# Last classic part of the down projection with tokens on the output partitions, the residual transposed between its products, and each token tile stored by itself

## The chip, the cores and the metric

The kernel runs on one core of one Trainium2 chip. The metric is the device time of one execution in microseconds (us), as the median of several runs. The kernel before took 2611.05 us (three runs: 2614.22, 2610.66, 2611.05).

## The reference, cut to what matters

One decoder layer for 512 tokens of width 2048, all in float32: an input projection, windowed attention and a gated short convolution, their merge, a cross-attention into 256 memory tokens, a SwiGLU mixer, and a last RMS norm. The lines that the change touches:

```python
h = h + memory_cross_attention(rms_norm(h, g_xattn[l]), mem_n, w_xq[l], w_xkv[l], w_xo[l])
# inside it: s = einsum('bshd,bmhd->bhsm', q, k) * X_HEAD_DIM ** -0.5
h = h + swiglu(rms_norm(h, g_ffn[l]), w_gate_up[l], w_down[l])   # (silu(g) * u) @ w_down, D_FF = 5632
return rms_norm(h, g_final)    # h * rsqrt(mean(h*h) + 1e-6) * g_final
```

## The kernel before, in words

**Arithmetic.** Almost every product is done in three fp32r matmuls: each operand is split into a high part (a copy that ScalarE, ACT, writes as fp32r) and a low part (the rest, which VectorE, DVE, subtracts), and hi·hi + hi·lo + lo·hi are added up in PSUM. `hi()` and `lo()` do this for weights in four slots of 128x512 (`w_hi`, `w_lo`, `SPL = 4`). The raw weights come in loads of 512 KB into four buffers (`raw`); a load waits until the low parts of the load four before it are done (`s_lo`). ACT and DVE each work through one list in order, so an instruction that waits holds everything behind it. SyncE (SP) issues the loads, also in order; GpSimd (POOL) issues spills and the accumulating stores of the residual. The large projections use a Strassen-like scheme of seven products on halves (`products`, `cycle_products`, L1025 and L1036), the rest the classic form (`columns`, L785 to L787; `rows`, L800 to L802).

**Start.** The tokens are transposed by TensorE (PE), tile by tile: call m of `x_in` (L839) transposes four 128x128 blocks into a bank; ACT copies it (`x_hi`, L1235), DVE subtracts (`x_lo`, L1853). Eight of these stand before the first product; ACT and DVE do six of them, then the first weight, then two more. The first product waits for all eight (`s_xlo`).

**Cross-attention.** The queries `xq_t` and keys `kx` are held in plain f32. Sixteen scores of 128x256 (`x_scores`, L1112) are each one f32 matmul, which the trace shows as two records. They stand between the products of the value projection.

**Down projection.** The 44 tiles of the hidden dimension are taken as 4 + 16 + 4 + 16 + 4. The parts of 4 are classic (`classic_part`), the parts of 16 go through the seven products (`down[0]`, `down[1]`). For the latter SP loads blocks of weights into `braw` (two buffers; the first lies over `raw`). Results of all parts but the last are added to `acc_dram` by accumulating stores that POOL issues. The last classic part has its features on the output partitions, 16 tiles of 128 features x 512 tokens, in four groups (`G_LAST` to `G_LAST + 3`) of four banks.

**End.** SP reloads the summed residual (`acc_end`, four loads of 1 MB) and POOL loads the final gain (`gfin`, 1 MB). DVE adds each finished bank to its tile (`last_sum`, L2664), ACT squares it, DVE adds the squares (L2318); four small matmuls sum them over the partitions (L816), ACT and DVE form the reciprocal root (L1812 to L1818, L1248), then 64 transposes on PE (L1200) turn the sum to tokens on partitions, DVE multiplies by root and gain from PSUM (L2695, 16 times) and SP stores eight pieces of 512 KB (L685).

Of the kernel before, what the change touches and what calls it, by code (L numbers as in the profile page):

```python
# [176 lines left out]
def build(nc, x, mem, g_mix, w_in, conv_w, sinks, w_attn_o, w_conv_o, w_out, g_xattn, g_mem,  # L177
          w_xq, w_xkv, w_xo, g_ffn, w_gate_up, w_down, g_final, rope, out):
    with ExitStack() as ctx:
# [45 lines left out]
        kx = at("kx", 168 * KB, [P, XH, NMEM])  # L225
# [16 lines left out]
        y_out = at("y_out", 0, [P, TT, D])  # L242
# [71 lines left out]

        def evicted(n, j):

            return (gate_t, up_t)[j // 2][:, n % 2, j % 2, :]
# [17 lines left out]
        X_STEPS = {-3: (6, 7), 7: (8, 9), 8: (10, 11), 11: (12, 13), 12: (14, 15)}  # L335
# [18 lines left out]
        s_mem = sem("mem_loaded")  # L354
        s_gfin = sem("gfinal_loaded")
# [48 lines left out]
        s_mtlo = sem("mem_lo_ready")  # L404
        s_xs = sem("xscores_done")
# [10 lines left out]
        s_shi = sem("combination_hi_ready")  # L416
# [5 lines left out]
        s_gn = sem("gate_scaled")  # L422
        s_un = sem("up_scaled")
# [39 lines left out]
        s_mshi = sem("mixer_combination_hi_ready")  # L463
# [12 lines left out]
        s_fT = sem("final_transposed")  # L476
        s_y = sem("y_ready")
        s_out = sem("out_stored")
# [8 lines left out]
        def _(sp):  # L487
# [162 lines left out]

            for i in range(3):
# [4 lines left out]
                if i == 2:  # L656
                    for c in range(2):
                        for p in range(2):
                            sp.wait_ge(s_add[p], 32 * (9 + c))
                        sp.wait_ge(ffn.used, down[1].number("P6", DB - 1) + 2)  # L660
                        sp.dma_start(acc_end[:, 4 * c:4 * c + 4, :], acc_dram[c]).then_inc(s_ald[c], 16)
                    for p in range(RAW, 8):
                        down_load(i, p)
                    for c in range(2, 4):
                        for p in range(2):
                            sp.wait_ge(s_add[p], 32 * (9 + c))
                        sp.wait_ge(ffn.used, down[1].number("P7", DB - 1) + 2)
                        sp.dma_start(acc_end[:, 4 * c:4 * c + 4, :], acc_dram[c]).then_inc(s_ald[c], 16)
                    continue
                for n in (0, 2, 1, 3):  # L670
                    quad_load(i, n)
                for p in range(RAW, 8):
                    down_load(i, p)
                    if p == 5:
                        for q in (1, 0, 2, 3):
                            down_block_load(i, 1, q)
                for q in range(4):
                    down_block_load(i, 0, q)
                for b in range(2, DB):
                    for q in (1, 0, 2, 3):  # L680
                        down_block_load(i, b, q)
            for m in range(2 * TT):
                t, f = m // 2, slice((m % 2) * (D // 2), (m % 2 + 1) * (D // 2))
                sp.wait_ge(s_y, 2 * (m + 1))
                sp.dma_start(out[0, t * P:(t + 1) * P, f], y_out[:, t, f]).then_inc(s_out, 16)  # L685
            sp.wait_ge(s_out, 16 * 2 * TT)
# [3 lines left out]
        def _(pool):  # L690
# [77 lines left out]
            pool.dma_start(gfin[:, :], g_final.partition_broadcast(P)).then_inc(s_gfin, 16)  # L768
# [3 lines left out]
        def _(pe):  # L772
# [69 lines left out]
            for m in range(8):  # L842
                x_in(m)
                if m == 3:
# [13 lines left out]
            for g in range(2):  # L858
                for k in range(KT):
                    wait_block(B_QKV + KT * g, 0, None, k)  # L860
                    if k == 0:
                        pe.wait_ge(s_xlo, 8 * g + 8)
# [243 lines left out]
            def x_scores(u):  # L1106
                h, t = divmod(u, TT)
                if u == 0:
                    pe.wait_ge(s_freed, 4 * G_XK + 4)
# [64 lines left out]
            for i in range(3):  # L1174
                for c in range(4):
                    g = G_DOWN + 4 * i + c
                    free = blocks_freed((ffn, *down)[i], c) if c < 2 else freed(g)
                    for k in range(CK):
# [4 lines left out]
                        columns(banks(g), k, CK, act[:, 0, :], act[:, 1, :], wait_bank=free)  # L1183
                if i < 2:
                    products(down[i])


            FB = banks(G_LAST)
            square_sums(FB[0], 3 * KT)
            for m in range(TT * 4):  # L1190
                t, kg = divmod(m, 4)
                bk = bank[(m + 1) % 8] if FB is A else bank[(m + 5) % 8]
                if m >= 7:
                    pe.wait_ge(s_y, m - 7 if m > 7 else 1)
# [1525 lines left out]
```

## Time and profile before

| | |
|---|---|
| runs of the kernel | 2614.22, 2610.66, 2611.05 us |
| the profiled execution's own time | 2611.81 us |
| its span, first to last instruction | 2610.0 us |
| mean granted TensorE clock | 0.999 |
| PE busy | 2589.1 us (99%) |
| DVE, ACT, POOL busy | 2039.8 (78%), 1326.6 (51%), 96.8 us (4%) |
| DMA | 360.02 MB, mean 138 GB/s |

A start time in a row below counts from the start of the span. The duration of a matmul is its latency; two that follow each other overlap, so the pace is read from the distance of their starts. A bracket at the end of a timeline row gives the idle time of the engine before it and what ended it. The profiled execution took 1.8 us more than its span and lies 0.76 us above the median.

### The profile page before, as it was taken

How to read it: one execution, taken by the hardware profiler on the slowest of the kernel's cores; microseconds unless marked ns; L12 is line 12 of the kernel's file. 1: busy time of each engine (PE TensorE's matmuls, PEld its weight loads, DVE VectorE, ACT ScalarE, POOL GpSimd, SP SyncE). 2: the span in 40 equal slices, each digit the busy share in tenths (PEclk: the TensorE clock that was granted, in tenths of full speed). 3: DMA queues.
4: the chain of work that ended last, by engine and by line, in shares of the span. 5: the costliest groups of instructions: out<-in, count | busy, mean ns of one | idle time of the engine just before them, and what ended most of it. 6: DMA issues, size and time to landing. Idle time of an engine off the chain costs nothing.

```text
span 2610.0 us, 36693 instructions
## 1 busy us (share of the span) xinstructions
PE 2589.1 (99%) x13649; PEld 2229.1 (85%) x13649; DVE 2039.8 (78%) x3362; ACT 1326.6 (51%) x2457; POOL 96.8 (4%) x154
## 2 busy tenths in 40 slices
PE   8999999999999999999999999999999999999998
PEld 7888888888888888888888888888888888888887
DVE  5556876654999974456879999999999998888886
ACT  6334554444555553435565555555555556456453
POOL 0000000000000000000000000000000001011100
PEclk9999999999999999999999999999999999999999
DMA  7332222545544573234434343343443467678664
GB/s 230 102 89 81 81 76 87 188 144 167 149 144 142 165 250 130 90 95 131 162 113 122 117 137 110 118 137 109 121 134 110 124 204 174 135 193 198 132 176 151
DMA packets 391715, 360.02 MB, mean 138 GB/s; under 512 B 11804, under 2 KB 314996, under 8 KB 388980
## 3 DMA queue, kind: packets, MB, share of 16 engines
q1 hardware_dynamic: 373620, 292.67, 37.9%
q0 software_dynamic: 17920, 65.02, 9.0%
q8 instruction: 109, 1.79, 0.3%
q14 instruction: 66, 0.54, 0.1%
HBM read 304.17 MB, written 53.48 MB: 137 GB/s over the span
## 4 chain that ended last, share of the span: by engine, by line
PE 96%; DVE 2%; DMA 1%; ACT 0%; issue 0%; DVEq 0%; ACTq 0%
PE bank L1025 35%; PE bank L1036 18%; PE bank L785 11%; PE bank L786 11%; PE bank L787 11%; PE bank L800 2%; PE bank L802 2%; PE bank L801 2%; PE bank L906 0%; DMA braw<-in_w_down_dram 0%; DMA h_both<-hidden_spilled 0%; DVE y_out L2695 0%; DVE s_both L2584 0%; PE bank L839 0%; PE bank L894 0%; PE bank L1140 0%
## 5 line engine op out<-in xcount | busy, mean ns | idle before, releaser
L2100 DVE TENSOR_TENSOR w_lo<-braw,w_hi 128x512 fp32r<-128x512 f32 x504 | 322.9, 683 | 21.6 <-ACT w_hi L1404 21.6
L1404 ACT ACTIVATE w_hi<-braw 128x512 fp32r<-128x512 f32 x504 | 285.5, 625 | 52.5 <-PE bank L1036 19.6
L1827 DVE TENSOR_TENSOR w_lo<-raw,w_hi 128x512 fp32r<-128x512 f32 x224 | 154.2, 690 | 201.8 <-ACT w_hi L1219 201.1
L1219 ACT ACTIVATE w_hi<-raw 128x512 fp32r<-128x512 f32 x224 | 141.5, 632 | 287.5 <-PE bank L787 282.6
L1829 DVE SCALAR_TENSOR_TENSOR w_lo<-raw,par,w_hi 128x512 fp32r<-128x512 f32 x208 | 155.1, 750 | 149.1 <-ACT w_hi L1219 148.0
L2100 DVE TENSOR_TENSOR h_both<-braw,h_both 128x512 fp32r<-128x512 f32 x392 | 250.9, 683 | 2.7 <-ACT h_both L1404 2.5
L1219 ACT ACTIVATE w_hi<-raw,par 128x512 fp32r<-128x512 f32 x208 | 149.3, 721 | 193.5 <-PE bank L787 122.4
L1404 ACT ACTIVATE h_both<-braw 128x512 fp32r<-128x512 f32 x392 | 221.9, 625 | 23.6 <-PE bank L1036 17.6
L785 PE MATMUL bank<-h_both,w_hi 128*128 128x512 f32 x576 | 228.9, 397 | 0.3 <-DVE v_c L1986 0.3
L786 PE MATMUL bank<-h_both,w_hi 128*128 128x512 f32 x576 | 224.8, 390 | 0.0
L787 PE MATMUL bank<-h_both,w_lo 128*128 128x512 f32 x576 | 224.6, 390 | 0.0
L1025 PE MATMUL bank<-s_both,w_hi 128*128 128x512 f32 x896 | 220.6, 391 | 0.0
L1025 PE MATMUL bank<-s_both,h_both 128*128 128x512 f32 x896 | 220.5, 391 | 0.0
L1427 ACT ACTIVATE snap_b<-bank 128x512 f32<-128x512 f32 x68 | 40.7, 599 | 323.7 <-PE bank L1025 321.7
L1025 PEld LDWEIGHTS bank<-s_both,h_both 128*128 128x128 f32 x896 | 164.7, 188 | 31.8
L1025 PEld LDWEIGHTS bank<-s_both,w_hi 128*128 128x128 f32 x896 | 164.5, 188 | 31.7
L1025 PE MATMUL bank<-h_both 128*128 128x512 f32 x672 | 167.5, 391 | 0.0
L1025 PE MATMUL bank<-h_both,w_hi 128*128 128x512 f32 x672 | 167.4, 391 | 0.0
L1025 PEld LDWEIGHTS bank<-h_both,w_hi 128*128 128x128 f32 x672 | 122.8, 188 | 23.3
L1025 PEld LDWEIGHTS bank<-h_both 128*128 128x128 f32 x672 | 122.6, 188 | 23.1
L787 PEld LDWEIGHTS bank<-h_both,w_lo 128*128 128x128 f32 x576 | 108.1, 188 | 23.7
L1036 PE MATMUL bank<-s_both,w_lo 128*128 128x256 f32 x896 | 125.5, 283 | 1.3 <-DVE w_lo L2100 1.3
(303 smaller groups left out, 5605.1 us busy)
## 6 DMA issues: line engine op xcount, KB each, us to landing
braw<-in_w_gate_up_dram SPq DMA_DIRECT2D x160, 512.0 KB, 5.2
raw<-in_w_in_dram SPq DMA_DIRECT2D x80, 512.0 KB, 3.7
braw<-in_w_in_dram SPq DMA_DIRECT2D x64, 512.0 KB, 5.0
braw<-in_w_down_dram SPq DMA_DIRECT2D x64, 512.0 KB, 6.0
raw<-in_w_out_dram SPq DMA_DIRECT2D x32, 512.0 KB, 3.8
raw<-in_w_down_dram SPq DMA_DIRECT2D x24, 512.0 KB, 5.6
hidden_spilled<-up_t POOLq DMA_DIRECT2D x44, 256.0 KB, 5.6
raw<-in_w_attn_o_dram SPq DMA_DIRECT2D x16, 512.0 KB, 3.8
```

Of the source, the lines that this page charges most:

```text
L785: pe.matmul(o_, w_hi[:, s, c], hi, start=(k == 0), stop=False)
L786: pe.matmul(o_, w_hi[:, s, c], lo, start=False, stop=False)
L787: mm = pe.matmul(o_, w_lo[:, s, c], hi, start=False, stop=(k == n - 1))
L800: pe.matmul(bk[j][:, :], hi[:, c], w_hi[:, s, :], start=(k == 0), stop=False)
L801: pe.matmul(bk[j][:, :], hi[:, c], w_lo[:, s, :], start=False, stop=False)
L1025: mm = pe.matmul(r, st.slot_hi[st.slot(n + half)][:, q, :], both, start=(not on and half == 0 and q == 0), stop=(on_last == "wide" and hal ...
L1036: mm = pe.matmul(r[:, 1, :], st.slot_lo[st.slot(n + half)][:, q, :], u_h, start=False, stop=(on_last == "narrow" and half == 1 and q == 3) ...
L1219: nc.scalar.activation(w_hi[:, s, :], raw[:, n % RAW, (b0 + k) % 2, :], ACT.Copy, scale=sc).then_inc(s_hi, 1)
L1404: nc.scalar.activation(st.slot_hi[s], weights(name, b)[:, 4 * half:4 * half + 4, :], ACT.Copy).then_inc(st.hi, 1)
L1827: nc.vector.tensor_tensor(w_lo[:, s, :], src, w_hi[:, s, :], ALU.subtract).then_inc(s_lo, 1)
L1829: nc.vector.scalar_tensor_tensor(w_lo[:, s, :], src, g[:, k:k + 1], w_hi[:, s, :], ALU.mult, ALU.subtract).then_inc(s_lo, 1)
L2100: nc.vector.tensor_tensor(st.slot_lo[s], weights(name, b)[:, 4 * half:4 * half + 4, :], st.slot_hi[s], ALU.subtract).then_inc(st.lo, 1)
```

## The change

The core of it, the end of the kernel:

```diff
-        y_out = at("y_out", 0, [P, TT, D])
+        y_out = at("y_out", 96 * KB, [P, TT, D])
+        end_hi = at("end_hi", 0, [P, 3 * CK, 512], F32R)
+        end_lo = at("end_lo", 24 * KB, [P, 3 * CK, 512], F32R)
+        END = [(t, c) for c in range(4) for t in range(2)] + [(t, c) for t in (2, 3) for c in range(4)]
+        END_LAST = {6: 0, 7: 1, 11: 2}
+        END_ROWS = {4: (0,), 5: (1,), 6: (2,), 7: (3,), 8: (4,), 9: (5,), 10: (6, 7), 11: (8, 9), 12: (10, 11, 12), 13: (13, 14), 14: (15,)}
...
+            def end_products(i):          # PE
+                t, c = END[i]
+                if i < 6:
+                    ((first, 0), (first, 1), (first, 2), (second, 2), (first, 3), (second, 0))[i][0]((0, 1, 2, 2, 3, 0)[i])
+                else:
+                    pe.wait_ge(s_freed, 4 * G_LAST + i - 5)
+                ts = slice(t * P, (t + 1) * P)
+                for k in range(CK):
+                    wait_block(B_DOWN + CK * (8 + c), 0, None, k)
...
+                    pe.matmul(sums[i % 6][:, :], act[:, 0, ts], hi, start=(k == 0), stop=False)
+                    pe.matmul(sums[i % 6][:, :], act[:, 0, ts], lo, start=False, stop=False)
+                    mm = pe.matmul(sums[i % 6][:, :], act[:, 1, ts], hi, start=False, stop=(k == CK - 1))
+                mm.then_inc(s_done, 1)
+            def end_rows(i):              # PE
+                t, c = END[i]
+                pe.wait_ge(s_ald[c], 16)
+                if i < 2:
+                    second(3 if i == 0 else 1)
+                else:
+                    pe.wait_ge(s_rows, i - 1)
+                for q in range(4):
+                    mm = pe.transpose(rows_[i % 2][:, q * P:(q + 1) * P], acc_end[:, 4 * c + q, t * P:(t + 1) * P], ident[:, :])
+                mm.then_inc(s_fT, 1)
+            for i in range(16):
+                end_products(i)
+                for r in END_ROWS.get(i, ()):
+                    end_rows(r)
...
+            for i in range(16):           # ACT; before it: 12 copies into end_hi and the root's table
+                rows_copy(i)
+                if i:
+                    rows_square(i - 1)
+                if i - 1 in END_LAST:
+                    root(5 + END_LAST[i - 1], ...)
+                if i - 2 in END_LAST:
+                    for c in range(4):
+                        rows_scale(END_LAST[i - 2], c)
+            rows_square(15)
+            root(8, rcol[:, 3:4], rtm[:, 3:4])
+            for c in range(2):
+                rows_scale(3, c)
...
+            for i in range(16):           # DVE; before it: 12 subtractions into end_lo, wait for gfin
+                rows_sum(i)
+                if i:
+                    dve.wait_ge(s_sqr, 2 * KT + i)
+                    link(rows_gain(i - 1, y_part(i - 1)))
+                if i - 1 in END_LAST:
+                    rows_rstd(END_LAST[i - 1])
+            rows_gain(15, tile4[:, 3, :])
+            dve.wait_ge(s_sqr, 2 * KT + 16)
+            rows_rstd(3)
+            dve.wait_ge(s_rcol, 7)
+            nc.vector.tensor_scalar(y_part(14), y_part(14), rcol[:, 3:4], None, ALU.mult).then_inc(s_y3, 1)
+            nc.vector.tensor_scalar(y_part(15), tile4[:, 3, :], rcol[:, 3:4], None, ALU.mult).then_inc(s_y3, 1)
...
+            for t in range(TT - 1):       # SP
+                sp.wait_ge(s_y, 4 * t + 4)
+                sp.dma_start(out[0, t * P:(t + 1) * P, :], y_out[:, t, :]).then_inc(s_out, 16)
+            for c in (2, 0, 3, 1):        # four stores of 256 KB for the last tile
```

`rows_copy(i)` copies the transposed residual of piece i (128 tokens x 512 features) from PSUM to `y_out`, `rows_sum(i)` adds the finished bank, `rows_square(i)` squares it with a row sum, `rows_gain(i)` multiplies it by `gfin`, `rows_rstd(t)` forms the reciprocal root of one token tile, `rows_scale(t, c)` multiplies a piece by it. A transposed piece goes into one of two banks, and `end_rows(i)` waits until `rows_copy(i - 2)` is done. A product from the seventh on waits for `rows_sum(i - 6)`.

The other edits: SP issues the residual's reloads behind the weight loads of the last part (weight load 4; 5, residual 0; 6, residual 1; 7, residual 2; residual 3), where before residual 0 and 1 stood ahead of weight loads 4 to 7. In the two earlier classic parts, the loads of block 1 of the following stage, which stood between weight loads 5 and 6, now stand behind those of block 0. At the start four of the eight `x_hi`, `x_lo` stand before the first weight and the other four behind one weight each (`X_FIRST`); the first product waits for five, and each fourth k for one more; the gains' transpose stands behind the second `x_in` in place of the fourth. In the cross-attention ACT and DVE split the queries and the keys into high and low parts (`xq_hi`, `xq_lo`, `kx_hi`, `kx_lo`; four 128x512 and four 128x256 on each engine) and a score is three fp32r matmuls:

```diff
-                pe.matmul(B[u % 4][:, 0:NMEM], xq_t[:, h, t * P:(t + 1) * P], kx[:, h, :],
-                          start=True, stop=True).then_inc(s_xs, 1)
+                pe.matmul(o_, xq_hi[:, h, q], kx_hi[:, h, :], start=True, stop=False)
+                pe.matmul(o_, xq_hi[:, h, q], kx_lo[:, h, :], start=False, stop=False)
+                pe.matmul(o_, xq_lo[:, h, q], kx_hi[:, h, :], start=False, stop=True).then_inc(s_xs, 1)
```

ACT's four `kx_hi` stand behind its second weight of the value projection, DVE's four `kx_lo` where the four copies `kx` stood, behind its third weight. Four semaphores are folded into others with their counts shifted.

## Rows read from the trace of the kernel before

**Rows 1.** Page, part 1: busy time and share of the span.
```profile
PE 2589.1 (99%) x13649; PEld 2229.1 (85%) x13649; DVE 2039.8 (78%) x3362; ACT 1326.6 (51%) x2457; POOL 96.8 (4%) x154
```
**Rows 2.** Waits of PE after 20 us (us in total, times, longest), the two longest.
```profile
PE bank L816 <- DVE ssq L2318: 3.5, 1, 3.5
PE bank L1036 <- DVE w_lo L2100: 1.3, 1, 1.3
```
**Rows 3.** Timeline (start, duration, engine), PE: first and last product of the part.
```profile
2545.73 0.40 PE L785 MATMUL bank<-s_res,w_hi 128*128 128x512 f32 x1
...
2589.65 0.39 PE L787 MATMUL bank<-s_res,w_lo 128*128 128x512 f32 x1
...
2594.72 8.57 PE L1200 MATMUL bank<-ident,acc_end 128*128 128x128 f32 x64
```
**Rows 4.** Timeline, the end: DVE; then SP's stores (first and last start).
```profile
2594.89 0.16 DVE L1812 TENSOR_SCALAR rtm<-bank 128x4 f32<-128x4 f32 x1 [1.41 <-PE bank L816]
...
2596.33 10.63 DVE L2695 SCALAR_TENSOR_TENSOR y_out<-bank,rcol,gfin 128x512 f32<-128x512 f32 x16
...
L685 SPq DMA_DIRECT2D out_dram<-y_out x8: 332/332/338, 2597.8 to 2607.0; - x8
```
**Rows 5.** Timeline, PE: eight transposes between two products at the start.
```profile
25.45 0.39 PE L802 MATMUL bank<-w_hi,h_both 128*128 128x512 f32 x1
...
25.68 1.03 PE L839 MATMUL bank<-ident,x_nat 128*128 128x128 f32 x8
...
26.78 0.39 PE L801 MATMUL bank<-w_lo,h_both 128*128 128x512 f32 x1
```
**Rows 6.** DMA issues, 2550 to 2555, then 2546 to 2550: KB, us to landing.
```profile
raw<-in_w_down_dram SPq DMA_DIRECT2D x1, 512.0 KB, 6.9
...
gfin<-in_g_final_dram POOLq DMA_DIRECT2D x1, 1024.0 KB, 9.2
```
**Rows 7.** Timeline, ACT: copies from PSUM, copies with a column scale, a table load.
```profile
2391.44 1.08 ACT L1668 ACTIVATE up_t<-bank 128x512 f32<-128x512 f32 x2
...
13.40 1.95 ACT L1219 ACTIVATE w_hi<-raw,par 128x512 fp32r<-128x512 f32 x3
...
2586.34 1.28 ACT L1794 ACT_TABLE_LOAD   x1
```
**Rows 8.** Groups by form: the squares of the end.
```profile
L1538 ACT ACTIVATE tile<-acc_end 128x512 f32<-128x512 f32 x16 | 10.1, 632 | 14.7 <-DVE acc_end L2664 14.6
```
**Rows 9.** Timeline, DVE: three linked 128x512 operations, each waiting for the one before.
```profile
2585.57 2.28 DVE L2318 TENSOR_TENSOR ssq<-ssq,tile 128x512 f32<-128x512 f32 x3
```
**Rows 10.** Windows: length, busy PE, PEld, DVE, ACT, POOL, granted clock, DMA share, GB/s.
```profile
2594.00:2595.00 1.00, 1.00 (x8) 1.00 (x8) 0.11 (x1) 0.00 (x0) 0.00 (x0) 0.58 0.00 0
...
2596.00:2597.00 1.00, 1.00 (x7) 1.00 (x6) 0.93 (x3) 0.00 (x0) 0.00 (x0) 0.50 0.00 0
2597.00:2598.00 1.00, 1.00 (x9) 1.00 (x8) 1.00 (x3) 0.00 (x0) 0.00 (x0) 0.71 0.00 0
...
15.00:16.00 1.00, 1.00 (x6) 0.83 (x5) 1.00 (x3) 0.35 (x1) 0.00 (x0) 1.00 0.66 240
```
**Rows 11.** Timeline at the start: PE's first product, DVE's last two subtractions before it.
```profile
14.67 0.47 PE L800 MATMUL bank<-w_hi,h_both 128*128 128x512 f32 x1 [2.66 <-DVE h_both L1853]
...
13.24 1.28 DVE L1853 TENSOR_TENSOR h_both<-bank,h_both 128x512 fp32r<-128x512 f32 x2
```
**Rows 12.** Timeline, cross-attention: scores, the product behind them, DVE's key copies, narrow matmuls.
```profile
1195.98 1.02 PE L1112 MATMUL bank<-kx,xq_t 128*128 128x256 f32 x4
...
1197.08 0.40 PE L801 MATMUL bank<-w_lo,mem_t 128*128 128x512 f32 x1
...
1193.48 1.41 DVE L2371 COPY kx<-bank 128x256 f32<-128x256 f32 x4
...
2392.59 1.11 PE L1036 MATMUL bank<-s_both,w_lo 128*128 128x256 f32 x8
```
**Rows 13.** Start of down[1]: DVE's wait; its load's landing; ACT's first use of block 1.
```profile
2392.07 1.23 DVE L2115 TENSOR_TENSOR braw<-braw 128x1024 f32<-128x1024 f32 x1 [2.53 <-DMA braw<-in_w_down_dram]
...
braw<-in_w_down_dram SPq DMA_DIRECT2D x1, 512.0 KB, 11.6
...
2396.25 2.18 ACT L1404 ACTIVATE w_hi<-braw 128x512 fp32r<-128x512 f32 x4
```

More of the change, by code:

```diff
@@ L656, in _ @@
                 if i == 2:
[L657 to L668, printed above, removed]
+                    for c in range(4):
+                        down_load(i, RAW + c)
+                        if c == 0:
+                            continue
+                        residual_load(c - 1)
+                    residual_load(3)
                     continue
@@ L1172, in _ @@
             products(ffn)
-            for i in range(3):
+            for i in range(2):
                 for c in range(4):
@@ L1183, in _ @@
                         columns(banks(g), k, CK, act[:, 0, :], act[:, 1, :], wait_bank=free)
-                if i < 2:
[L1185 to L1194, printed above, removed]
-                if m == 7:
-                    pe.wait_ge(s_rcol, 4)
-                if m >= 8:
-                    pe.wait_ge(s_y, m - 7)
+                products(down[i])
@@ L1585, in _ @@
                     mem_hi(7)
+                if 4 <= k < 8:
+                    act.wait_ge(s_freed, 4 * G_XQ + k - 3)
+                    nc.scalar.activation(xq_hi[:, k - 4, :], xq_t[:, k - 4, :], ACT.Copy).then_inc(s_xh, 1)
             def x_exp(u):
@@ L1602, in _ @@
                 hi(B_XV, G_XV, k, gm)
+                if k == 1:
+                    for j in range(4):
+                        act.wait_ge(s_done, 4 * G_XK + j + 1)
+                        nc.scalar.activation(kx_hi[:, j, :], banks(G_XK)[j][:, 0:NMEM], ACT.Copy).then_inc(s_xh, 1)
                 for u in x_units(k - 4):
@@ L1795, in _ @@
-            for j in range(4):
-                f_sq(3)(j)
-            root(5, rcol[:, :], rtm[:, :])
+            for n in range(SPL, 4 * CK):
+                m = B_DOWN + 2 * 4 * CK + n
+                if n == SPL:
+                    act.wait_ge(ffn.used, down[1].halves())
+                if n % 2 == 0:
+                    act.wait_ge(s_raw[m // 2 % RAW], 16 * (m // 2 // RAW + 1))
+                nc.scalar.activation(end_hi[:, n - SPL, :], raw[:, m // 2 % RAW, m % 2, :], ACT.Copy).then_inc(s_hi, 1)
@@ new lines, in rows_scale @@
+            def rows_scale(t, c):
+                act.wait_ge(s_rcol, 4 + t)
+                y = y_out[:, t, 512 * c:512 * c + 512]
+                nc.scalar.activation(y, y, ACT.Copy, scale=rcol[:, t:t + 1]).then_inc(s_y, 1)
+            for i in range(16):
[3 more added lines that the diff above has]
+                if i - 1 in END_LAST:
+                    root(5 + END_LAST[i - 1], rcol[:, END_LAST[i - 1]:END_LAST[i - 1] + 1], rtm[:, END_LAST[i - 1]:END_LAST[i - 1] + 1])
+                if i - 2 in END_LAST:
+                    for c in range(4):
+                        rows_scale(END_LAST[i - 2], c)
@@ L2369, in kx_out @@
             def kx_out(j):
-                done(G_XK, j)
-                nc.vector.tensor_copy(kx[:, j, :], banks(G_XK)[j][:, 0:NMEM]).then_inc(s_freed, 1)
+                dve.wait_ge(s_xh, XH + j + 1)
+                nc.vector.tensor_tensor(kx_lo[:, j, :], banks(G_XK)[j][:, 0:NMEM], kx_hi[:, j, :],
+                                        ALU.subtract).then_inc(s_freed, 1)
             def x_max(u):
```

172 lines of the change are left out of this document (92 added, 80 removed).

## The prediction

> **What bounds the kernel now.** I read the page's busy times first: PE is busy 2589.1 of 2610.0 us [rows 1]. Then the waits of PE: behind the first 20 us it waits 3.5 us once, in the end, and 1.3 us once, in down[1] [rows 2]. So no stage is worth anything unless PE's own work there changes; the reader is to look for gaps of PE, and there are three: the start, the 1.3 us, and the end. Third came the timeline of the end. The part's 192 matmuls start from 2545.73 to 2589.65, 0.23 us apart, and are over at 2590.04 [rows 3]. From there to 2610.0 are 20.0 us in which PE computes nothing that the reference asks for: sums and squares to 2594.9, the root to 2596.33, then 16 DVE multiplications of 0.66 us [rows 4] beside the 64 transposes. A bank of four transposes takes PE less than 0.66, so DVE sets that pace. After the last multiplication (2606.96) the last 512 KB take 3.0 us.
>
> **The end, step by step.** The change keeps the 192 matmuls (16 pieces of 12, 2.75 us each). It removes from behind them the 64 transposes, most of the multiplications and seven of eight large stores, and puts the transposes between the products.
>
> *Transposes on PE.* Eight between two products: from 25.45 to 26.78 are 1.33 us where two paces of 0.23 would stand, so 0.87 us [rows 5]: 0.095 for one and 0.11 for the change of kind. 16 groups of four in 11 places: 16 x 0.38 + 11 x 0.11 = 7.3 us, all on PE's path. Bounds 6 and 9.
>
> *First wait: the seventh product.* It needs the weights of the fourth column block and a bank that rows_sum(0) frees. PE would be there at 2545.73 + 6 x 2.75 + 2 x 0.49 = 2563.2. On ACT, rows_copy(0) is behind the last of the 12 weight copies, and that is behind weight load 7. The load goes out at about 2551.2 (when DVE's low parts allow it), behind 1 MB of residual 0, load 6 and 1 MB of residual 1 in SP's queue, and beside the gain's load, which alone took 9.2 us, and in whose company a load of 512 KB took 6.9 [rows 6]. With 6.9 it lands at 2558; if the 3.5 MB of SP's queue share the engines with the gain and the last adds, at 2564. I take 2561, the middle. Then two copies (1.2), the root's table that now lies ahead of rows_copy(0) (1.28 + 0.2) [rows 7], the copy 0.6 and the sum 0.7: the bank is free at 2565.0, a stall of 1.8 us. Bounds 0 and 4.8.
>
> *Second wait: the two banks of transposed pieces.* This is the step I trust most. Piece 11 waits for rows_copy(9), piece 12 for rows_copy(10), and ACT has to work through its list in between. From the start of rows_copy(8) to the end of rows_copy(10) it does: copy 0.5, square 0.63 [rows 8], then root(1), which waits for DVE's root chain of tile 0 (1.0), sum 8 (0.6), gain 7 (0.80, linked, [rows 9]) and reduce and variance (0.36), together 2.0 us of waiting; the root 0.25; four scalings at 0.615 (three copies with a column scale start within 1.95 - 0.72 us) = 2.46; copy 0.5, square 0.63, four scalings 2.46, copy 0.5. Copies from PSUM follow each other at 0.5 [rows 7]. The sum is 9.9 us. PE in that time, from the end of transposes 8 on: transposes 9 (0.38), product 12 (2.75), transposes 10 and 11 (0.87): 4.0 us. So PE stalls 5.9 us, in two pieces of about 3 us with one group of transposes between them, and 0.4 more because rows_copy(8) itself comes behind root(0). I take 6.3; bounds 5 and 7.5, by how much of DVE's 2.0 is hidden. Nothing makes it up: three products and four groups (9.8 us) follow on PE, and ACT's and DVE's rest of the list is about as long.
>
> *The clock.* The granted clock was still 1.00 after PE's idle 2.66 us at the start [rows 10, 11]; after the 3.5 us of the end it was 0.58 and then 0.50, the lower of the two levels, and back by 2598, some 3.2 us later [rows 2, 10]. Two idle pieces of 3 us with 0.4 us between them lie nearer to the second. A fall costs 3.2 us at half pace, 1.6 us of products, of which ACT and DVE hide 0.4. I take 1.2, bounds 0 and 3.3 (two falls).
>
> The last matmul then ends at 2590.04 + 7.3 + 1.8 + 6.3 + 1.2 = 2606.6.
>
> *Behind it.* DVE: sum 15 (0.6), gain 14 (0.80), gain 15 (0.68), reduce (0.2): 2.3 us; from the variance to the first scaled value 1.44 us (2594.89 to 2596.33); one piece of 0.65: 4.4 us. ACT's square (0.63) and its two scalings lie beside that. Then four stores of 256 KB in place of one of 512 KB: 3.0 us plus another 0.5 MB at the pace of the eight stores, 1.31 us each [rows 4]: 4.3. Together 8.7 us where 20.0 stood. The store of tile 2 is out by then. The span would end at 2615.3: the end alone is 5.3 us slower. It wins 11.3 us behind the last matmul and pays 16.6 ahead of it.
>
> **The start.** The last two x_lo (1.28 us) no longer stand before the first product, and ACT's order saves one copy pitch of 0.53: 1.8 us of the 2.66 that PE idled [rows 11]. DVE then has 1.35 us of work per k for four k, PE 1.37, so no later stall. Bounds: 0 and 2.66 (PE's own transposes end at 12.0). If it holds, everything behind moves up: -1.8.
>
> **The cross-attention.** Two f32 scores cost 1197.08 - 1195.98 - 0.23 = 0.87 us; six fp32r matmuls of 256 at 0.12 (eight in 1.11, of which the last 0.28) cost 0.73 [rows 12]. 16 scores: -1.1. Against it, the first score waits for kx_lo: ACT's four kx_hi end at about 1193.9 (PE finishes the last key bank at 1193.4), its third weight at 1194.6, DVE's at 1195.4, then four subtractions as long as the copies (1.41): 1196.8, 0.8 later than PE is there. Net -0.3; bounds -1.1 and +1.5. The added splits of the queries fit in: ACT 1.3, DVE 1.4 of PE's 1.45 us per k.
>
> **The block loads.** In down[1] DVE waited until 2392.07 for the last load of block 0, which took 11.6 us to land, and this is where PE's 1.3 us come from [rows 2, 13]. With 2 MB of block 1 out of the way before it, it can land some 2 us sooner: up to -1.3. But block 1 now comes behind it, four loads of about 2 us, so its first part lands near 2394 to 2396, and ACT reads it at 2396.25 [rows 13]. I take -1.0; bounds -1.3 and +4 (both stages late). The folded semaphores and the moved gains' transpose (its latest time, PE at 9.5, is before PE is needed) cost nothing.
>
> **A rule beside it.** On the first wait, "DMA: Bandwidth & Descriptors" of the Trainium skill, "Queues, rings and completion order", says that each DMA engine takes packets in turn from the queues that have work. By that rule SP's queue gets half of the engines while the gain loads, and load 7 would land near 2564, not 2561: 3 us more. The trace's 6.9 us beside the gain agrees in kind; nothing in it shows 3.5 MB queued there.
>
> **The sum.** +5.3 - 1.8 - 0.3 - 1.0 = +2.2 us. The profiled execution was 2611.81, 0.76 above the median; against the median of 2611.05 I predict 2613.2. A measurement of this kernel can tell about 0.2% (5.2 us): 2605.8 and 2616.3 are the bounds of "same".
>
> **Rivals.**
> *The copies keep up.* If ACT were two pieces ahead at transposes 11 and 12, the 6.3 and 1.2 us fall away: 2605.7, and 2603.9 if load 7 is early too. For it: ACT is busy only 51% of the kernel. Against it: its list is strictly in order, and copy 8 can't start before transposes 8. 14%.
> *The late weights decide (other side).* Load 7 lands at 2564 or later; the seventh product stalls 4.8 us or more, and from a landing of 2559.2 on every us costs one. The clock falls there or twice: 2613.2 + 3.0 + 2.1 = 2618.3. For it: 7 MB go at that time, and at the stores' 1.31 us for 0.5 MB [rows 4] they fill 18 us. Against: the gain may be nearly done when load 6 goes. 18%.
> *Every wait costs a cold stretch.* Each of the three waits of PE is followed by products at the lower clock: three times 1.6 us in place of 1.2 in all, 2616.8. For it speaks the 3.5 us case, against it that the 2.66 us at the start left the clock at 1.00 [rows 10, 11]. 8%. "TensorE: Matmul & The Clock Gate" of the Trainium skill, "Why this matters for your kernels", warns of idle gaps between bursts of matmuls in this sense.
> *Block 1 late.* PE stalls at P1 of block 1 in both stages: +5.0 over my term, 2618. 6%.
> The forecast has 54%.
>
> **Range and chances.** 2607.0 to 2618.5: the bounds of the forecast's terms, most of the late weights, and a part of the copies that keep up. Faster 0.13, same 0.63, slower 0.24.
>
> **What would show it.** PE waiting at the seventh product for rows_sum, and at transposes 11 and 12 for rows_copy, some 6 us together behind four scalings on ACT; the granted clock below 1 near 2595; the first product at 12.8 us; a first score that waits for kx_lo; last matmul at about 2602 (all moved up by 3 us), 8.7 us before the end. Wrong if PE passes transposes 11 and 12 without a wait, if load 7 lands far from 2561, or if down[0] or down[1] shows a new wait for braw.

## The result and the profile after

The changed kernel takes 2618.99 us (median of its nine runs, eight of them from 2617.3 to 2620.44) against 2611.05: the ratio is 1.003, with a 95% interval of 1.0021 to 1.0039. It is slower by 7.9 us, more than the 0.2% that a measurement of this kernel can tell, and 0.5 us above the range. The profiled execution was 2618.83, its span 2616.9 against 2610.0, so it shows 6.9 of the 7.9 us. The one run outside these took 11042.25 us at a mean granted clock of 0.63, which nothing here explains; the ratio leaves it out.

The waits of TensorE in the changed kernel, behind its first for x (line waited for, us in total, times, longest), answer to [rows 2]. Before, the long one was 3.5 us and lay behind the last product; now 11.0 us lie between the products:

```profile
PE bank L1236 <- DVE y_out L2762: 5.5, 1, 5.5
PE bank L1250 <- ACT y_out L1858: 5.5, 2, 2.9
PE bank L829 <- DVE h_both L1943: 1.1, 1, 1.1
PE bank L1145 <- DVE kx_lo L2461: 0.5, 1, 0.5
```

The timeline of TensorE: the first product at the start, the first and the last matmul of the last part (compare [rows 3, 11]).

```profile
12.15 0.47 PE L829 MATMUL bank<-w_hi,h_both 128*128 128x512 f32 x1 [1.08 <-DVE h_both L1943]
...
2540.91 0.40 PE L1236 MATMUL bank<-w_hi,s_res 128*128 128x512 f32 x1
...
2607.48 0.39 PE L1238 MATMUL bank<-end_hi,s_res 128*128 128x512 f32 x1
```

The reader is to take three differences from these rows. The part begins 4.8 us earlier (2545.73 to 2540.91). From its first to its last matmul it takes 66.57 us where it took 43.92: +22.65. From the end of the last matmul (2607.87) to the end of the span are 9.0 us where 20.0 stood: -11.0. The sum, -4.8 + 22.65 - 11.0, is the +6.9 of the span.

**The first wait.** What SP issues in the changed kernel (start, duration), and then the landings of the two weight loads (6, then 7), of those that start near 2545.15 and near 2546.36 (KB, us from issue to landing):

```profile
2545.15 0.37 SPq L662 DMA_DIRECT2D raw<-in_w_down_dram  x1
2545.64 0.53 SPq L681 DMA_DIRECT2D acc_end<-residual_spilled  x1
2546.36 0.37 SPq L662 DMA_DIRECT2D raw<-in_w_down_dram  x1
```
```profile
raw<-in_w_down_dram SPq DMA_DIRECT2D x1, 512.0 KB, 9.8
...
raw<-in_w_down_dram SPq DMA_DIRECT2D x1, 512.0 KB, 13.5
```

Load 7 is out at 2546.36, where the forecast had it (2551.2 on before's scale, less 4.8), but it needs 13.5 us, not 9.8. It lands at 2559.9, and ScalarE, VectorE and TensorE go on from there:

```profile
2559.92 1.15 ACT L1850 ACTIVATE end_hi<-raw 128x512 fp32r<-128x512 f32 x2 [3.74 <-DMA raw<-in_w_down_dram]
2561.09 1.28 ACT L1851 ACT_TABLE_LOAD   x1
...
2562.49 1.07 ACT L1858 ACTIVATE y_out<-bank 128x512 f32<-128x512 f32 x2
```
```profile
2560.58 1.29 DVE L2755 TENSOR_TENSOR end_lo<-raw,end_hi 128x512 fp32r<-128x512 f32 x2 [3.60 <-ACT end_hi L1850]
2563.16 1.28 DVE L2762 TENSOR_TENSOR y_out<-y_out,bank 128x512 f32<-128x512 f32 x2 [1.29 <-issue]
```
```profile
2554.55 0.60 PE L1250 MATMUL bank<-ident,acc_end 128*128 128x128 f32 x4
...
2557.76 0.60 PE L1250 MATMUL bank<-ident,acc_end 128*128 128x128 f32 x4
2563.90 0.79 PE L1236 MATMUL bank<-end_hi,s_res 128*128 128x512 f32 x1 [5.55 <-DVE y_out L2762]
```

The two copies at 2562.49 are those of pieces 0 and 1. Piece 0, whose sum frees the bank that TensorE waits for, was transposed at 2554.55 and done at 2555.15; it lay there for 7.3 us, until ScalarE, which waited for weights that the copy doesn't need, came to it.

**The second wait.** TensorE's transposes 10, 11 and 12, and ScalarE's list in that time:

```profile
2589.17 0.60 PE L1250 MATMUL bank<-ident,acc_end 128*128 128x128 f32 x4
2592.33 0.63 PE L1250 MATMUL bank<-ident,acc_end 128*128 128x128 f32 x4 [2.57 <-ACT y_out L1858]
2595.88 1.09 PE L1250 MATMUL bank<-ident,acc_end 128*128 128x128 f32 x4 [2.91 <-ACT y_out L1858]
```
```profile
2589.16 2.54 ACT L1873 ACTIVATE y_out<-y_out,rcol 128x512 f32<-128x512 f32 x4
2591.61 0.57 ACT L1858 ACTIVATE y_out<-bank 128x512 f32<-128x512 f32 x1
2592.09 0.62 ACT L1866 ACTIVATE tile<-y_out 128x512 f32<-128x512 f32 x1
2592.61 0.19 ACT L1866 ACTIVATION_READ_ACCUMULATOR tile<-y_out 128x1 f32 x1
2592.70 2.55 ACT L1873 ACTIVATE y_out<-y_out,rcol 128x512 f32<-128x512 f32 x4
2595.16 0.58 ACT L1858 ACTIVATE y_out<-bank 128x512 f32<-128x512 f32 x1
```

Four scalings of 0.61 us stand ahead of each copy that TensorE waits for.

**The clock.** Windows of 1 us: length, busy share of PE, PEld, DVE, ACT, POOL, then the granted clock, DMA share, GB/s.

```profile
2562.00:2563.00 1.00, 0.00 (x0) 0.00 (x0) 0.00 (x0) 0.99 (x4) 0.00 (x0) 0.55 0.94 393
...
2567.00:2568.00 1.00, 1.00 (x4) 0.75 (x3) 0.00 (x0) 0.00 (x0) 0.00 (x0) 0.50 0.00 0
2569.00:2570.00 1.00, 1.00 (x8) 0.82 (x7) 0.00 (x0) 0.29 (x1) 0.00 (x0) 1.00 0.00 0
2592.00:2593.00 1.00, 0.63 (x4) 0.42 (x4) 0.78 (x2) 1.00 (x4) 0.00 (x0) 0.91 0.57 238
2593.00:2594.00 1.00, 0.00 (x0) 0.00 (x0) 0.53 (x1) 1.00 (x3) 0.00 (x0) 0.50 1.01 418
2598.00:2599.00 1.00, 1.00 (x4) 0.76 (x3) 0.96 (x2) 0.60 (x2) 0.00 (x0) 0.50 0.67 270
```

The clock falls to the lower of its two levels twice: within the first wait, and with the transposes between the two pieces of the second. Product 7 starts at 2563.90, and the next transposes come at 2569.08: 5.2 us for work that takes 2.75 at the upper level.

**The tail.** VectorE behind the last matmul:

```profile
2608.01 0.69 DVE L2762 TENSOR_TENSOR y_out<-y_out,bank 128x512 f32<-128x512 f32 x1 [0.97 <-PE bank L1238]
2608.61 0.69 DVE L2768 TENSOR_TENSOR y_out<-y_out,gfin 128x512 f32<-128x512 f32 x1
2609.33 0.69 DVE L2768 TENSOR_TENSOR tile<-y_out,gfin 128x512 f32<-128x512 f32 x1
...
2611.51 0.49 DVE L2788 TENSOR_SCALAR y_out<-y_out,rcol 128x512 f32<-128x512 f32 x1
```

### The profile page after: what moved, and what is told of

Read it like the earlier page. It is cut to its first block, busy times and chain, and to the rows that moved or that the text cites. A ratio compares the mean times of both kernels' runs of the same rounds, so it can differ in the third digit from the quotient of the medians.

```text
span 2616.9 us, 36810 instructions
## 1 busy us (share of the span) xinstructions
PE 2588.6 (99%) x13657; PEld 2228.3 (85%) x13657; DVE 2035.6 (78%) x3374; ACT 1347.7 (52%) x2514; POOL 97.0 (4%) x154
## 4 chain that ended last, share of the span: by engine, by line
PE 97%; DVE 1%; ACT 1%; DMA 1%; issue 0%; ACTq 0%; DVEq 0%
PE bank L1056 35%; PE bank L1067 18%; PE bank L814 11%; PE bank L815 11%; PE bank L816 11%; PE bank L829 2%; PE bank L831 2%; PE bank L830 2%; DMA raw<-in_w_down_dram 1%; PE bank L937 0%; PE bank L1236 0%; PE bank L1237 0%; PE bank L1238 0%; PE bank L925 0%; PE bank L1174 0%
## 5 line engine op out<-in xcount | busy, mean ns | idle before, releaser
L1917 DVE TENSOR_TENSOR w_lo<-raw,w_hi 128x512 fp32r<-128x512 f32 x212 | 146.0, 691 | 185.2 <-ACT w_hi L1274 184.3
L1274 ACT ACTIVATE w_hi<-raw 128x512 fp32r<-128x512 f32 x212 | 134.2, 633 | 274.9 <-PE bank L816 270.2
L1056 PEld LDWEIGHTS bank<-h_both,w_hi 128*128 128x128 f32 x672 | 122.8, 188 | 23.3
L814 PEld LDWEIGHTS bank<-h_both,w_hi 128*128 128x128 f32 x576 | 108.2, 188 | 21.3 <-issue 0.5
```

Of the source, the lines that this page charges most:

```text
L814: pe.matmul(o_, w_hi[:, s, c], hi, start=(k == 0), stop=False)
L1056: mm = pe.matmul(r, st.slot_hi[st.slot(n + half)][:, q, :], both, start=(not on and half == 0 and q == 0), stop=(on_last == "wide" and hal ...
L1274: nc.scalar.activation(w_hi[:, s, :], raw[:, n % RAW, (b0 + k) % 2, :], ACT.Copy, scale=sc).then_inc(s_hi, 1)
L1917: nc.vector.tensor_tensor(w_lo[:, s, :], src, w_hi[:, s, :], ALU.subtract).then_inc(s_lo, 1)
```

## The experiments

Two theories stood at the beginning. *Queued behind the weights*: the 5.5 us are a copy and a sum that stand, in the order of ScalarE's and VectorE's lists, behind weight copies that wait for load 7; the second wait is the eight scalings; the clock follows both. *Transfer alone*: load 7 is so late that the product would wait as long in any order. Each kernel was compared with the kernel before on the same chip. An interval reaches some 2.4 us to either side, so between two rows of the table a difference of less than about 3 us is not shown by the times; what tells such rows apart are the columns of the traces, and each trace is one execution (e1's took 2.0 us more than e1's median, e4's 1.2 less). The table takes from each profiled execution when the last part's first matmul starts, the time to its last matmul, the waits of TensorE in it, and the rest over 51.26 us (explained below), which but for some 0.3 us is what the lower clock cost (e4 and e12 have 0.2 and 0.3 without a fall of the clock in the part); "tail" is from the last matmul's end to the end of the span.

| kernel | median us | ratio, 95% | first | part | 1st wait | 2nd wait | rest | tail |
|---|---|---|---|---|---|---|---|---|
| changed | 2618.99 | 1.0021 to 1.0039 | 2540.91 | 66.57 | 5.55 | 5.48 | 4.3 | 9.0 |
| e1 load order | 2615.76 | 1.0007 to 1.0026 | 2542.85 | 63.58 | 3.13 | 5.47 | 3.7 | 9.1 |
| e2 gain late | 2615.60 | 1.0008 to 1.0027 | 2542.49 | 61.07 | 2.84 | 5.02 | 2.0 | 9.1 |
| e3 scale on DVE | 2614.84 | 1.0004 to 1.0023 | 2542.91 | 60.54 | 5.59 | 1.13 | 2.6 | 10.6 |
| e4 both | 2609.54 | 0.9985 to 1.0004 | 2541.16 | 54.15 | 1.59 | 1.11 | 0.2 | 10.6 |
| e8 sum first too | 2606.59 | 0.9976 to 0.9994 | 2541.00 | 52.38 | 0 | 1.12 | 0 | 11.0 |
| e9 sum first alone | 2614.43 | 1.0003 to 1.0021 | 2541.30 | 61.58 | 1.96 | 5.48 | 2.9 | 9.0 |
| e10 one transpose | 2604.86 | 0.9970 to 0.9988 | 2541.03 | 49.58 | 0 | 3.15 | - | 11.6 |
| e11 e8, ACT scales | 2612.07 | 0.9995 to 1.0013 | 2542.70 | 59.16 | 0 | 5.49 | 2.4 | 9.1 |
| e12 e8, old loads | 2608.85 | 0.9985 to 1.0003 | 2541.45 | 54.18 | 1.52 | 1.11 | 0.3 | 11.1 |

The 51.26 us are e8's 52.38 without its waits of 1.12: 16 products with the transposes between them at full clock. Before, the same products took 43.92, so the transposes cost 7.34.

**e1: the loads in another order.**

```diff
-for c in range(4):
-    down_load(i, RAW + c)
-    if c == 0: continue
-    residual_load(c - 1)
-residual_load(3)
+down_load(i, RAW); down_load(i, RAW + 1); residual_load(0)
+down_load(i, RAW + 2); down_load(i, RAW + 3)
+for c in range(1, 4): residual_load(c)
```

> The changed kernel with SP's weight loads 6 and 7 ahead of the reload of residual 1; nothing else. Theory (queue order): load 7 lands 13.5 us after its issue because 1 MB of residual 1 lies ahead of it; without it, it lands some 9 to 10 us after its issue, the seventh product waits 1 to 2 us in place of 5.5 and the granted clock does not fall there (2.4 us): 2619.0 - 6 = 2613. Rival (the gain's load alone slows it, the order does not matter): load 7 still lands over 12 us after its issue, the seventh product still waits 4.5 us or more: 2618 to 2619. The waits at transposes 11 and 12 stay at 5.5 us in both.

2615.76, 3.2 us less than the changed kernel, but 2.8 more than expected. Load 7 lands 11.1 us after its issue instead of 13.5 (load 6, as before, 9.8), and the first wait falls from 5.55 to 3.13 us, not to 1 or 2: 1 MB of residual less ahead of load 7 is worth 2.4 us. The clock still falls behind this wait. The second wait stays as it is.

```profile
raw<-in_w_down_dram SPq DMA_DIRECT2D x1, 512.0 KB, 11.1
```

**e2: the gains' load behind the weights.** GpSimd waits for load 7 before it issues the 1 MB of gains, and VectorE waits for them before the first multiplication instead of before the first sum.

```diff
+last_raw = (B_DOWN + 2 * 4 * CK) // 2 + 7
+pool.wait_ge(s_raw[last_raw % RAW], 16 * (last_raw // RAW + 1))
 pool.dma_start(gfin[:, :], g_final.partition_broadcast(P))
...
-dve.wait_ge(s_mem, 32)
 for i in range(16):
     rows_sum(i)
+    if i == 1:
+        dve.wait_ge(s_mem, 32)
```

> The changed kernel with POOL's load of the gain held back until weight load 7 has landed, and DVE's wait for it moved ahead of the first multiplication by the gain; SP's order is the changed kernel's. Theory (engines shared between the two queues): load 7 lands 7 to 9 us after its issue in place of 13.5, the seventh product waits under 1 us and the clock does not fall there: 2619.0 - 8 = 2611. Rival (only the order in SP's queue counts): load 7 lands 12 us or more after its issue, 2618 or more.

2615.60, 4.6 us more than expected. Load 7 lands after 10.9 us instead of 13.5 (load 6 after 8.3 instead of 9.8), and the first wait is 2.84. Neither branch of the expectation gave this: the gains of the other queue cost load 7 2.6 us, about as much as the residual ahead of it, and no run took both away. After this wait the clock stayed at 1.00; after e1's 3.13 it fell. The load's landing in e2, then the windows of e2 and of e1 behind the wait:

```profile
raw<-in_w_down_dram SPq DMA_DIRECT2D x1, 512.0 KB, 10.9
```

```profile
2563.00:2564.00 1.00, 1.00 (x5) 0.82 (x5) 0.32 (x1) 0.47 (x2) 0.00 (x0) 1.00 1.01 426
```
```profile
2564.00:2565.00 1.00, 1.00 (x5) 0.81 (x4) 0.69 (x1) 0.12 (x2) 0.00 (x0) 0.82 0.94 393
```

In the traces e2's part is 2.5 us shorter than e1's, by this fall and by shorter waits. In the medians the two agree within 0.2; e1's profiled execution lies 2.0 us above its median and e2's 0.7 below, and what the clock did in their other executions is not shown. Further on in e2 the clock fell within a wait of only 2.56 us, the first piece of the second wait, and the transposes behind it took 1.09 us instead of 0.63:

```profile
2588.00:2589.00 1.00, 0.13 (x1) 0.16 (x2) 0.24 (x1) 1.00 (x3) 0.00 (x0) 0.67 0.00 0
```
```profile
2588.87 1.09 PE L1252 MATMUL bank<-ident,acc_end 128*128 128x128 f32 x4 [2.56 <-ACT y_out L1860]
```

**e3: tiles 0 to 2 are scaled on VectorE**, in one operation with the gains, at most two pieces behind each sum; ScalarE only copies, squares and takes the roots.

```diff
-for c in range(4):
-    rows_scale(END_LAST[i - 2], c)
...
+nc.vector.scalar_tensor_tensor(y, y, rcol[:, t:t + 1], gfin[:, f], ALU.mult, ALU.mult)
```

> The changed kernel with the 12 scalings of token tiles 0 to 2 taken from ACT's list: DVE multiplies by root and gain in one operation, at most two behind each sum, in place of 12 multiplications by the gain; ACT keeps only the two scalings of tile 3. Theory (PE waits at transposes 11 and 12 because the copies stand behind eight scalings on ACT): PE waits under 2 us there in place of 5.5, the granted clock does not fall near 2593 (2 us): 2619.0 - 6 = 2613. Rival (DVE's root chain sets the copies' pace, the scalings lie beside it): the waits stay at 4 us or more, 2617 to 2619. The wait of the seventh product, 5.5 us, stays in both.

2614.84, 1.8 us more than expected. The waits at the banks of transposed pieces fall from 5.48 to 1.13 us, and no clock falls there; but VectorE, which has more to do, makes the tail 1.5 us longer. The first wait stays at 5.59, with its cold stretch. The waits of e3's last part:

```profile
PE bank L1236 <- DVE y_out L2759: 5.6, 1, 5.6
PE bank L1250 <- ACT y_out L1858: 1.1, 2, 0.7
```

**e4: e1 and e3 together**, and the root's table loaded six weight copies into the list instead of behind all of them (ScalarE idles there for a load in any case).

```diff
 for n in range(SPL, 4 * CK):
+    if n == SPL + 6:
+        nc.scalar.activation(rtm2[:, :], rmem[:, :], ACT.Sqrt)
...
-nc.scalar.activation(rtm2[:, :], rmem[:, :], ACT.Sqrt)
```

> Both edits, SP's loads 6 and 7 ahead of residual 1 and the scalings on DVE, and the table load of the root moved between ACT's sixth and seventh weight copy of the part. If the two waits and their two falls of the clock are all that the end pays (5.5 + 2.4 + 5.5 + 2.0 us), and they add up: 2619.0 - 15 = 2604, faster than the kernel before by 0.2 to 0.3%. Rival (what is taken out of one wait comes back in another, since ACT's and DVE's lists are as long as PE's): 2609 or more.

2609.54, not to be told from the kernel before. The first wait is 1.59: e1's 3.13 less the 1.5 us of the table load and the operation that calls it. With both waits small there is no cold stretch before TensorE is done. The expected 2604 is missed by 5.5 us: of the 15.3 us of waits and clock 2.9 are left, and the tail is 1.6 longer. The rest of the miss lies ahead of the part and between the profiled execution and the median. So the rival's time came out (2609 or more), and of its mechanism a part: work taken from one list comes back at the end of another.

**e5, e6, e7: the front alone.** e7 is the kernel before with the edits of the start; e6 adds the cross-attention's and the folded semaphores; e5 adds the order of the block loads. All three keep the old ending.

```diff
-X_STEPS = {-3: (6, 7), 7: (8, 9), 8: (10, 11), 11: (12, 13), 12: (14, 15)}
+X_FIRST = {0: (4,), 1: (5,), 2: (6,), 3: (7,)}      # e7, e6, e5
...
-pe.matmul(B[u % 4][:, 0:NMEM], xq_t[...], kx[:, h, :], start=True, stop=True)
+pe.matmul(o_, xq_hi[:, h, q], kx_hi[:, h, :], ...)  # e6, e5: three products
...
-    if p == 5:                                      # e5
-        for q in (1, 0, 2, 3): down_block_load(i, 1, q)
```

> The kernel before with the edits of the start alone. By the first product's place in the changed kernel's trace (12.15 against 14.67) 2608.5 to 2609; what is then left between it and the run with all edits of the front is the cross-attention's. The rival, that the early start is paid back by later waits of the first group's products on their tiles, gives 2610 to 2611.

2608.06, ratio 0.9990 (0.9981 to 0.9999), 2.3 us less than its kernel before (2610.34). The forecast of this expectation was too careful, its rival wrong. The first product starts at 12.35:

```profile
12.35 0.47 PE L801 MATMUL bank<-w_hi,h_both 128*128 128x512 f32 x1 [0.45 <-DVE h_both L1856]
```

> As the run before, but with the block loads left in the old order. If the order of the block loads does nothing, the two agree within 0.5 us; if the old order costs the wait of 2.5 us before DVE's first block copy in the last stage, this one is 1 to 1.3 us slower.

> The kernel before with every edit of the change but those of the last classic part: the start (the first products after 4 of the 8 transposed tiles), the cross-attention scores in three single-pass products, and the block loads of both down projections in their new order; the ending is the old one. If the front edits carry what the changed kernel's trace shows (first product 2.5 us earlier, scores 1.2 us shorter, the first product of the last part 4.8 us earlier), it takes 2606 to 2607.5. The rival: the gain of the front is only the profiled runs' scatter, and it takes 2609 or more.

2607.95 and 2608.17. The order of the block loads does nothing, as expected; that the front is worth 4 us was wrong. In the traces e7's part begins at 2541.50, e6's at 2540.91 and e5's at 2541.09, so some 0.4 to 0.6 us are the cross-attention's; the medians differ by 0.1, which these runs can't tell from none. The 1.3 us wait in down[1] [rows 2], which the changed kernel's trace lacks, is absent from e6 and e7 too, which have the old order, and is back in e1 and e3 (1.3) and e2 and e11 (1.0), which have the new one. So it doesn't go by the order. In e1 VectorE waits 2.4 us for a load there, as it waited 2.53 in the kernel before [rows 13]; what makes this load late in some executions stays open. e1's wait of TensorE:

```profile
PE bank L1068 <- DVE w_lo L2191: 1.3, 1, 1.3
```

**e8: e4 and three moves more.**

```diff
 for n in range(SPL, 4 * CK):                        # ScalarE; VectorE in the same way
+    if n == 4 * CK - 2:
+        rows_copy(0)                                # VectorE: rows_sum(0)
...
-dve.wait_ge(s_mem, 32)
+    if i == 7: dve.wait_ge(s_mem, 32)
...
-rows_sum(15); rows_gain(14, ...)
+rows_gain(14, ...); rows_sum(15)
```

> The changed kernel with its loads reordered and tiles 0 to 2 scaled on DVE, as in the run that did both, and with three moves more: ScalarE's first copy of transposed rows and VectorE's first sum stand ahead of the last two weight copies, VectorE waits for the gains at their first use, and its multiplication for part 14 stands ahead of the last sum. If the seventh product waits for the sum behind the last weight copies, its wait of 1.6 us goes and the tail is 0.6 shorter: 2607 to 2608. If the seventh product waits for its own weights as much as for the sum, the wait stays at 1 us or more and the time is 2608.5 to 2609.5.

2606.59 (2606.31 to 2607.97), ratio 0.9985 (0.9976 to 0.9994): 12.4 us less than the changed kernel, 0.15% less than the kernel before, with an interval that leaves out 1, and the lowest median of a complete kernel here. It is 0.4 below what was expected. ScalarE copies the first rows between the copies of loads 6 and 7, and the seventh product doesn't wait:

```profile
2555.10 1.15 ACT L1857 ACTIVATE end_hi<-raw 128x512 fp32r<-128x512 f32 x2 [7.66 <-DMA raw<-in_w_down_dram]
2556.15 0.58 ACT L1854 ACTIVATE y_out<-bank 128x512 f32<-128x512 f32 x1
2557.52 1.15 ACT L1857 ACTIVATE end_hi<-raw 128x512 fp32r<-128x512 f32 x2 [0.79 <-DMA raw<-in_w_down_dram]
```

The tail, expected 0.6 us shorter than e4's 10.6, is 11.0 us (9.0 in the changed kernel). TensorE's last matmul starts at 2593.38, but VectorE, which now does the scalings, is behind and begins the last sum only at 2596.32:

```profile
2593.38 0.39 PE L1239 MATMUL bank<-end_hi,s_res 128*128 128x512 f32 x1
```
```profile
2592.73 1.42 DVE L2788 SCALAR_TENSOR_TENSOR y_out<-y_out,rcol,gfin 128x512 f32<-128x512 f32 x2
2594.06 0.68 DVE L2758 TENSOR_TENSOR y_out<-y_out,bank 128x512 f32<-128x512 f32 x1
...
2596.32 0.69 DVE L2758 TENSOR_TENSOR y_out<-y_out,bank 128x512 f32<-128x512 f32 x1
```

**e9: the sum first, nothing else.** In the changed kernel, only `rows_copy(0)` and `rows_sum(0)` move ahead of weight copies 14 and 15, as in the first hunk of e8.

> The changed kernel with one move alone: ScalarE's first copy of transposed rows and VectorE's first sum stand ahead of the last two weight copies (14 and 15, which come with weight load 7). Loads and scalings are as in the changed kernel. If the wait of 5.5 us is that of a sum queued behind copies that wait for load 7, the seventh product starts at once, and what is left is its own need of the last weights, copied at 2562 to 2564 against a need at about 2560.4: some 2 to 3.5 us of waiting instead of 5.5, and 2615.5 to 2617. If load 7 is late enough to hold the product whatever the order of the copies, the time is that of the changed kernel, 2618.5 to 2619.

2614.43, 4.6 us less than the changed kernel from a move of two instructions. Load 7 is as late as it was: it lands 13.4 us after its issue. The seventh product starts at once and then waits 1.49 us inside itself for the last weights' low parts; the eighth waits 0.47 for the second sum:

```profile
2561.63 0.50 PE L1236 MATMUL bank<-end_hi,s_res 128*128 128x512 f32 x1 [1.49 <-DVE end_lo L2766]
...
2564.20 0.50 PE L1236 MATMUL bank<-end_hi,s_res 128*128 128x512 f32 x1 [0.47 <-DVE y_out L2759]
```

The theory of the transfer alone falls: with the late load in place, 3.6 of the 5.55 us of waiting belong to the order of the lists. The other 1.96 are the product's own need of the late weights. The time is 1 us below what was expected, because the clock stayed at 1.00 behind these two short waits, which the expectation had left out.

**e10: one transpose in place of four** in each of the 16 groups of e8; three quarters of the residual are left out, so the kernel shows only a time.

```diff
-for q in range(4):
+for q in range(1):
     mm = pe.transpose(rows_[i % 2][:, q * P:(q + 1) * P], acc_end[...], ident[:, :])
```

> The run with the reordered loads, DVE's scalings and the first sum ahead, with one transpose of 128x128 in each of the 16 groups instead of four; three quarters of the residual rows are left out, so that its time shows what 48 transposes cost TensorE. By the rows of the run it is made from (a group of four puts the next product's first matmul 0.35 us later and its second another 0.09) 48 transposes at 0.11 us each are 4.9 to 5.3 us: 2601.3 to 2601.8. If the transposes partly fill time in which the products would wait for ScalarE's copies in any case, less than 4 us goes: 2602.6 or more.

2604.86, only 1.7 us less than e8 (2.2 by the spans), though its part without waits is 49.58 - 3.15 = 46.43 us, 4.83 less than 51.26. So a transpose costs TensorE 0.10 us, as the forecast had it. But of the 4.83 us 2.0 turn into more waiting for ScalarE's copies (3.15 against 1.12), and 0.6 into a longer tail: behind a shorter TensorE stand the lists of the other two engines.

**e11: e8 with the scalings back on ScalarE** (loads, table and first sum as in e8).

> The changed kernel with the reordered loads, the table load early and the first sum ahead, but ScalarE scales tiles 0 to 2 as in the changed kernel. If the second wait (2.6 and 2.9 us at transposes 11 and 12) and the clock that falls with it belong to the scalings alone, it is back in full: 4.4 us more waiting than with DVE's scalings, and up to 3 us of half clock, 2611 to 2613.5. If a front without the first wait moves PE so far ahead that it waits more, above 2613.5; if the first wait had caused the second, 2607.5 or less.

2612.07, inside what the first theory gave. The second wait is back in full, 5.49 us, without a first one; so the first did not cause it. The part is 6.8 us longer than e8's: 4.4 of waiting and 2.4 of half clock. The tail gives 2.0 back.

**e12: e8 with the changed kernel's order of loads.**

> The run with DVE's scalings and the first sum ahead, but with the weight and residual loads in the order of the changed kernel. If the sum's place is what mattered and the order of the loads only moved it, the seventh product waits 1.5 to 3.5 us inside itself for the last weights, and it takes 2608.5 to 2611; if the order of the loads is the larger part of the 5.5 us, 2611.5 or more; if it matters nothing once the sum is ahead, 2606.6.

2608.85, 2.3 us above e8, with a wait of 1.52 us for the last low parts. With the sum ahead, the order of the loads is worth some 2 us by the medians (the intervals overlap) and 1.52 us of waiting by the traces; with the sum behind, it was 3.2 and 2.4 (e1). Order of the lists and order of the loads both count, the first for more of the waiting: 3.6 us in e9 against 2.4 in e1. By the times alone, 4.6 against 3.2, that isn't shown.

## Why the prediction was wrong

**The step that failed is the size of the first wait**, given as 1.8 us (0 to 4.8) and measured as 5.55, and with it the clock, given as 1.2 (0 to 3.3) and measured as 4.3. Together they are 6.9 us too small; other terms, 2.2 us off the other way, left 4.7 us between the forecast of +2.2 and the traces' +6.9.

- *Transposes on PE*: 7.3 forecast, 7.34 measured (e8), and 0.10 us for one (e10). Right.
- *First wait*: the place and the chain behind it were right (last weight copies, table load, copy, sum), and so was the issue of load 7. Its landing was not: 13.5 us, 2564.7 on before's scale, where I had taken 2561 as the middle of 2558 and 2564. The reason for 2561 was a single row of 6.9 us beside the gains [rows 6], read in a stretch in which SP issued single weight loads and nothing of the residual. e1 and e2 show both shares: 2.4 us of wait for the residual ahead of it, 2.7 for the gains. The bound of 2564, where both queues share the engines, was 0.7 us off. "DMA: Bandwidth & Descriptors" ("Queues, rings and completion order") of the Trainium skill states the rule behind it, that each DMA engine takes turns, packet by packet, between the queues that have work for it. The trace agrees in the landing. That is the rival *the late weights decide*, and its 2618.3 is 0.7 from the median: it had 18%. It was that close in part by luck: it put 8.1 us on the first wait and the clock together, where 9.8 were measured, and the other terms made up the difference.
- What the forecast did not ask is whether the copy and the sum have to stand behind load 7 at all. e9 shows that they don't.
- *Second wait*: 6.3 forecast (5 to 7.5), 5.48 measured. The mechanism was the scalings, shown by e3 and e11. ScalarE idled 1.49 us for VectorE ahead of the root of tile 1, not 2.0.
- *The clock*: I took one fall, at the second wait, and 1.2 us; there were two, and the bound for two was 3.3. The first, which came with the long first wait, cost 2.4 us (5.2 for 2.75), the second the other 1.9. Nothing of it was hidden, as I had thought 0.4 to be. e11 has one fall and 2.4 us.
- *Tail*: 8.7 forecast, 9.0 measured. *Behind the last matmul* it wins 11.0 where 11.3 were said. Right.
- *The start*: -1.8 forecast; the first product is 2.5 us earlier, and e7 gives 2.3 us in the median. ScalarE's and VectorE's first pieces are in time for all of the gap but 1.1 us. *Cross-attention*: -0.3 forecast, -0.4 to -0.6 in the traces (the wait for kx_lo is 0.55, not 0.8), not measurable in the medians. *Block loads*: -1.0 forecast; the trace of the changed kernel has the 1.3 us, but e5 and e6 show that the edit is worth nothing. That term was right by luck. The feared wait for block 1 did not come.
- What I called the step that I trust most was right; the one that moved the result had the poorest row behind it. The chances reflected that too little: 18% for a case whose only condition was a landing time taken half way between two ends.

What the whole change would have been worth: its front gives 2.3 us (e7); its ending costs nearly 11 us as written (2618.99 against e5's 2608.17) and, once the two waits are gone, is 1.5 us ahead of the old one by the medians (e8 2606.59 against e7 2608.06 and e5 2608.17; their intervals overlap, so this last step is not shown).

## What to carry to other kernels

Where work that finishes a stage is threaded between products, list for each engine what stands ahead of the first piece that TensorE needs back, and take out what waits for a transfer: two instructions moved were worth 4.6 us here, with the same bytes loaded. Price a load by all bytes that are under way in the same 10 us, its own queue's and the other queues', and when a landing decides the sign, forecast from the late end. A wait within a dense stretch costs its length plus, when the clock falls, another 2.0 to 2.9 us behind it (e2, e3, e9 and e11, with one fall each). After an engine is relieved, look at once at who does its work at the end (here VectorE, tail 9.0 to 11.0).

## What the runs showed of the hardware

The granted clock was still 1.00 behind idle stretches of TensorE of 2.66 us at the start [rows 10, 11], of 2.84 (e2), and of 1.49 and 0.47 (e9). It fell behind those of 3.49 in the kernel before [rows 2, 10] and of 3.13 (e1), and within those of 5.55 and 5.59 (e3). But it also fell within one of 2.56 in e2, later in the same execution that stayed at 1.00 behind 2.84, and with or behind the one group of transposes between two waits of 2.57 and 2.9 (changed kernel, e1, e9, e11). So the length of a single wait did not decide it here; what did, no run shows.

The last weight load, 512 KB, took 13.5 us to land in the changed kernel, 10.9 without the gains beside it (e2) and 11.1 with 1 MB of residual moved behind it (e1); in the kernel before, one took 6.9 beside the gains [rows 6]. In e9 and e12 TensorE waited inside a product rather than ahead of it, and the profile then names the last low part, not the load, as the releaser: one has to follow VectorE's and ScalarE's rows back to the transfer.
